# Four weight slots, the low part written over the raw block, and one conversion instruction per block and engine

## The reference

```python
mod = (silu(c) @ w_mod[i] + b_mod[i]).reshape(-1, 3, 3, D_MODEL)      # D_MODEL = 1024
def _sublayer(x, fn, mod_j, g, b, weight):
    shift, scale, gate = mod_j[:, 0, None, :], mod_j[:, 1, None, :], mod_j[:, 2, None, :]
    y = fn(x * (1 + scale) + shift)
    return _layernorm(DEEPNORM_ALPHA * x + weight * gate * y, g, b)
def _swiglu(h, w_in, w_out):
    gate, up = jnp.split(h @ w_in, 2, axis=-1)
    return (jax.nn.silu(gate) * up) @ w_out
```

## Time and profile before

| | us |
|---|---|
| median of the three runs | 3140.94 |
| the profiled execution | 3138.93 |
| its span | 3137.1 |
| TensorE busy (matmuls) | 2776.5 |
| VectorE busy | 2017.5 |
| GpSimd busy | 1389.1 |
| ScalarE busy | 1265.3 |

### The profile page before, as it was taken

One profiled execution on the slowest core, in us unless ns is written; L12 is line 12 of the kernel. 1 busy time (PEld: TensorE's weight loads), 2 busy tenths in 40 slices (PEclk: granted clock), 3 DMA queues, 4 the chain that ended last, 5 costly groups with the idle time before them and its releaser, 6 DMA issues.

```text
span 3137.1 us, 53378 instructions
## 1 busy us (share of the span) xinstructions
PE 2776.5 (89%) x20695; PEld 2656.6 (85%) x20695; DVE 2017.5 (64%) x2628; ACT 1265.3 (40%) x1667; POOL 1389.1 (44%) x1170
## 2 busy tenths in 40 slices
PE   3998889999976999999889999999879969779797
PEld 3998789999965999999764899999769969479797
DVE  6667776676658766666666666765876564764654
ACT  2444344344333444444332344443434434244443
POOL 0693958469383583793920079277670000000000
PEclk7998889999887898998975899899889989689898
DMA  8764557577472575764730377567445545034452
GB/s 298 252 249 144 189 202 252 202 240 260 148 247 71 198 254 180 255 256 158 235 120 0 108 254 267 176 231 271 151 142 173 176 155 177 14 111 131 134 185 83
DMA packets 357173, 576.21 MB, mean 184 GB/s; under 512 B 22256, under 2 KB 297899, under 8 KB 356907
## 3 DMA queue, kind: packets, MB, share of 16 engines
q1 hardware_dynamic: 357034, 574.29, 53.2%
HBM read 573.20 MB, written 1.05 MB: 183 GB/s over the span
## 4 chain that ended last, share of the span: by engine, by line
PE 70%; DVE 16%; issue 6%; POOL 4%; ACT 2%; DMA 1%; SPq 1%; DVEq 0%; POOLq 0%; ACTq 0%
PE ps L1553 64%; DVE wlo L1011 3%; POOL mod_acc L639 3%; PE ps L1873 1%; DVE acc L1126 1%; PE ps L1864 1%; DVE acc L1042 1%; DVE z L1142 1%; POOL mod_w L634 1%; ACT whi L654 1%; DVE std L1148 1%; DVE prob L1243 1%; PE ps L1694 1%; DVE hf L1155 1%; POOL mod_acc L630 1%
## 5 line engine op out<-in xcount | busy, mean ns | idle before, releaser
L1011 DVE TENSOR_TENSOR wlo<-raw,whi 128x1024 fp32r<-128x1024 f32 x804 | 1132.6, 1420 | 851.5 <-ACT whi L654 850.7
L654 ACT ACTIVATE whi<-raw 128x1024 fp32r<-128x1024 f32 x804 | 838.1, 1050 | 1227.9 <-PE ps L1553 1153.0
L1553 PE MATMUL ps<-H_hi,whi 128*128 128x256 f32 x4256 | 1230.3, 289 | 97.0 <-DVE H_lo L1160 37.6
L1553 PE MATMUL ps<-H_lo,whi 128*128 128x256 f32 x4256 | 1225.3, 288 | 0.0
L1553 PE MATMUL ps<-H_hi,wlo 128*128 128x256 f32 x4256 | 1224.3, 288 | 0.0
L1553 PEld LDWEIGHTS ps<-H_hi,whi 128*128 128x128 f32 x4256 | 839.6, 197 | 103.2 <-issue 85.3
L1553 PEld LDWEIGHTS ps<-H_lo,whi 128*128 128x128 f32 x4256 | 839.7, 197 | 0.1
L1553 PEld LDWEIGHTS ps<-H_hi,wlo 128*128 128x128 f32 x4256 | 838.8, 197 | 0.0
L639 POOL TENSOR_TENSOR mod_acc<-mod_acc,mod_w 128x512 f32<-128x512 f32 x462 | 792.3, 1743 | 0.0
L625 POOL TENSOR_TENSOR pool_tick<-cond 128x1 f32<-128x1 f32 x176 | 129.8, 738 | 952.9 <-DVE ax L1054 761.7
L1553 PE MATMUL ps<-A_hi,whi 128*128 (+1 forms) x1880 | 536.1, 285 | 16.0 <-DVE wlo L1011 12.9
(11 more groups left out here) (276 smaller groups left out, 2257.3 us busy)
## 6 DMA issues: line engine op xcount, KB each, us to landing
raw<-in_ffn_w_in_dram SPq DMA_DIRECT2D x176, 1024.0 KB, 5.1
mod_w<-in_w_mod_dram SPq DMA_DIRECT2D x180, 768.0 KB, 6.0
raw<-in_ffn_w_out_dram SPq DMA_DIRECT2D x88, 1024.0 KB, 6.5
raw<-in_w_gate_up_dram SPq DMA_DIRECT2D x22, 1024.0 KB, 5.1
raw<-in_ssm_w_in_dram SPq DMA_DIRECT2D x20, 1024.0 KB, 6.8
raw<-in_w_in_dram SPq DMA_DIRECT2D x14, 1024.0 KB, 5.0
raw<-in_diff_w_in_dram SPq DMA_DIRECT2D x12, 1024.0 KB, 7.0
raw<-in_w_down_dram SPq DMA_DIRECT2D x11, 1024.0 KB, 4.9
```

Source lines behind the costliest of these rows:

```text
L654: return nc.scalar.activation(dst, src, ACT.Copy)
L1011: tt(wlo[b % 2][:, r], raw[b % RAW][:, r], whi[b % 2][:, r].bitcast(F32), ALU.subtract).then_inc(w_lo, 1)
L1553: m = pe.matmul(out, l, r, start=first and i == 0, stop=last and i == 2, skip_group_check=rest)
```

## The change

- `raw`, `wlo` and `whi` now have four slots each; `wlo` i lies at the address of `raw` i, so the subtraction writes over its own input. The memory used is the same.
- ScalarE and VectorE convert a block with one instruction of its whole width (2048 columns, 1152 for the q blocks of MLA, 256 for dt). ScalarE no longer waits for products. TensorE waits once per block for the low part.
- The load of block b waits for TensorE's products of block b-4 (before: for VectorE's split of block b-4).
- The first two blocks of the next step are converted in the last turns of `projected`, ahead of the layer norm; `finish` and the conversions inside `dve_ln` and `dve_pre` are gone.
- Loads on SyncE are written out instead of looped, and the units of modulation have new places: `mod_rows` gives the turn behind whose load each unit stands. The loads of the next step's first blocks are no longer pulled ahead of the last units of a mixer.

```diff
+def mod_rows(kind):
+    if kind == "mla":
+        turns = [1, 1, 5, 6, 7, 8, 10] + 9 * [12]
+    elif kind == "diff":
+        turns = [1, 1] + [3 + 5 * j // 4 for j in range(8)] + 6 * [15]
+    elif kind == "ssm":
+        turns = [1, 1] + [2 + 3 * j // 2 for j in range(14)]
+    else:
+        turns = [1, 1] + [2 + 2 * j for j in range(14)]
...
-        whi = [at(f"whi{i}", [P, SLOT], room(4 * SLOT), F32R) for i in range(2)]
-        wlo = [at(f"wlo{i}", [P, SLOT], room(4 * SLOT), F32R) for i in range(2)]
+        wlo = [at(f"wlo{i}", [P, SLOT], base + 4 * SLOT * i, F32R) for i in range(RAW)]
+        whi = [at(f"whi{i}", [P, SLOT], room(4 * SLOT), F32R) for i in range(RAW)]
...
                 if b >= RAW:
-                    sp.wait_ge(w_lo, 2 * (b - RAW + 1) if it is None else 2 * (b - RAW + 1) + 8 * it)
+                    sp.wait_ge(products, plan.used[b - RAW][1])
...
+            def load_mod(sub, unit):
+                k, half = divmod(unit, 2)
+                u = UNITS * sub + unit
+                sp.wait_ge(mod_used, u - 1)
...
+                    nxt = st.args[0] + 1 if st.kind not in ("hyb", "xatt") else SUB * DEPTH
+                    after = mod_rows(st.kind) if nxt < SUB * DEPTH else {}
+                    blocks = [b for g in st.lin.values() for b in range(g.b, g.b + g.n)]
+                    for i, b in enumerate(blocks):
+                        if b >= 2:
+                            load(b)
+                        for unit in after.get(i, []):
+                            load_mod(nxt, unit)
...
-                for h in range(2):
-                    if b >= 2:
-                        u = plan.used[b - 2][h]
-                        act.wait_ge(products, u if it is None else 4 * upb * it + u)
-                    r = slice(h * HALF, min((h + 1) * HALF, width))
-                    copy(whi[b % 2][:, r], raw[b % RAW][:, r]).then_inc(w_hi, 1)
+                r = slice(0, plan.width[b])
+                copy(whi[b % RAW][:, r], raw[b % RAW][:, r]).then_inc(w_hi, 1)
...
-                for h in range(2):
-                    v = 2 * b + h + 1
-                    dve.wait_ge(w_hi, v if it is None else 8 * it + v)
-                    r = slice(h * HALF, min((h + 1) * HALF, width))
-                    tt(wlo[b % 2][:, r], raw[b % RAW][:, r], whi[b % 2][:, r].bitcast(F32), ALU.subtract).then_inc(w_lo, 1)
+                dve.wait_ge(w_hi, b + 1 if it is None else 4 * it + b + 1)
+                r = slice(0, plan.width[b])
+                tt(wlo[b % RAW][:, r], raw[b % RAW][:, r], whi[b % RAW][:, r].bitcast(F32), ALU.subtract).then_inc(w_lo, 1)
...
-                walk(dve, g, lambda i, it: None if it is None and i >= g.n - 2 else convert(g.b + i + 2, it), 1, 2)
+                walk(dve, g, lambda i, it: convert(g.b + i + 2, it), 1, 2)
```

More of the change, by code:

```diff
@@ L182 @@
 }
+UNITS = 2 * DC
+def mod_rows(kind):
[7 more added lines that the diff above has]
+        turns = [1, 1] + [2 + 2 * j for j in range(14)]
+    after = {}
+    for u, t in enumerate(turns):
+        after.setdefault(t, []).append(u)
+    return after
 class Step:
@@ L201, in __init__ @@
         self.mods = SUB * DEPTH
-        self.blocks = []
+        self.blocks, self.width = [], []
         self.used = []
@@ L228, in block @@
         self.blocks.append(loads)
+        self.width.append({"dt": DC * SSM_H, "q_up": QUP}.get(loads[0][0], SLOT))
         self.slot[b % RAW] += 16 * len(loads)
@@ L564, in _ @@
                         sp.dma_start(mod_first[u % ring], w).then_inc(first_loaded[u % ring], 16)
[L565 to L587, removed]
+                if st.kind in ("ffn", "mla", "diff", "ssm", "hyb", "xatt"):
+                    nxt = st.args[0] + 1 if st.kind not in ("hyb", "xatt") else SUB * DEPTH
[6 more added lines that the diff above has]
+                            load_mod(nxt, unit)
+                    if st.kind == "ffn" and st.args[0] == SUB * DEPTH - 1:
                         sp.wait_ge(s["mod_sum"], st.n["mod_sum"])
@@ L590, in _ @@
                         sp.dma_start(mem[:, :, :], A["mem_2"][0].rearrange("(t p) d -> p t d", p=P)).then_inc(second_loaded, 16)
[L591 to L605, removed]
                 if st.kind == "store":
@@ L654, in copy, with convert @@
                 return nc.scalar.activation(dst, src, ACT.Copy)
[L656 removed]
+            def convert(b, it=None):
                 if b >= NB:
@@ L776, in turn @@
                 def turn(i, it=None):
-                    convert(g.b + i + 2, it, 2)
+                    convert(g.b + i + 2, it)
                     if i % 2 == 0:
@@ L789, in projected @@
                 g = st.lin["out"]
-                walk(act, g, lambda i, it: None if it is None and i == g.n - 1 else convert(g.b + i + 2, it, 2), 1, 2)
-            def finish(g):
-                convert(g.b + g.n + 1)
+                walk(act, g, lambda i, it: convert(g.b + i + 2, it), 1, 2)
             def act_mla(st, n):
@@ L1506, in dve_pre @@
             def dve_pre(st, n):
-                g = steps[steps.index(st) - 2].lin["out"]
                 fold(n, "squared")
-                convert(g.b + g.n)
                 dve.wait_ge(s["std"], n["std"] + 1)
@@ L1612, in turn @@
                             xh, xl = (x[:, ds(it * 8 + k, 1), :].rearrange("p a n -> p (a n)") for x in (x_hi, x_lo))
-                        m = three(ybank(g, c), b % 2, h * HALF + c * P, P, xh, xl, k == 0 and c % 2 == 0, last and h == 1, rest=True)
+                        m = three(ybank(g, c), b % RAW, h * HALF + c * P, P, xh, xl, k == 0 and c % 2 == 0, last and h == 1, rest=True)
                         if last and h == 1 or not last and c == DC - 1:
```

55 lines of the change are left out of this document (21 added, 34 removed).

## The result

The kernel after takes 3210.95 us (median of four runs, 3206.66 to 3211.20) against 3140.63 beside it on the same chip. The ratio is 1.0225, with an interval of 1.0205 to 1.0244. The forecast was 3216, range 3165 to 3255. The profiled execution took 3206.66 us, its span is 3204.8, and the mean granted clock 0.896.

A forecast was written before the change was run, and what follows sets the result against it. In feed-forwards, most of the span, TensorE's unbroken matmuls were taken as the bound, so more slots gain nothing. Terms 67 + 3 + 4 - 9 - 2 + 12 = +75 on 3138.93 gave 3214, on the median 3216; range 3165 to 3255.

The forecast's parts named there:

- The hold at block 3: Feed-forwards: unit 2's wait, now ahead of load 3, stalls TensorE; 11.2 us in each of six, 67 us.
- Sublayer 0: First feed-forward: `ax` is ready early, so block 3 is only 3 us late; +3 (0 to 6).
- My reason about halves: Block 3 of feed-forwards: with whole-block conversions TensorE can't start on half a block any more.
- The layer norms: Reciprocal 1.4 us earlier, sums 1.8 later: net +0.4 for nine norms; together with last norm and `pre` steps, +4.
- MLA: Two MLA sublayers: GpSimd starts and runs earlier, next step's loads land later; -4.6 each, together -9 (-20 to +5).
- The other step: MLA's end: next step's two loads stand behind unit 15, so centred `z` comes at +8.6 instead of +3.5, +5.1.
- The differential mixer: Earlier start (-2.3) and earlier `ax` against conversions in series, GpSimd's pace holding as before; -2 (-10 to +8).
- The SSM: Hold 11 us, later loads meeting fewer units give some 4 back, whole-block xbc conversions cost 5; +12 (-5 to +25).
- The sum: Whole kernel: 67 + 3 + 4 - 9 - 2 + 12 = +75 us.
- half a hold: Rival: GpSimd slips ahead of the conversion or load 3 lands in 5 us; 3177, chance 0.21.
- more serial cost: Rival, also "the serial rival": whole-block conversions in series cost another 35 us in mixers and norms; 3250, chance 0.12.
- the third: Rival without a hold: unit 0 used by about T+6.2, feed-forwards cost nothing; 3135, chance 0.11.

The follow-up runs named there:

- experiment 5: Kernel after with feed-forward units 2 and 3 behind loads 5 and 7, the others two blocks apart from there: 3144.81 us, ratio 1.0025.
- experiment 4: Kernel before with only the feed-forwards' modulation units at the change's places: 3210.34 us, ratio 1.0234.
- experiment 1: Kernel after with feed-forward unit 2 behind load 4 instead of load 2: 3170.55 us, ratio 1.0116; second version, behind load 3: 3177.59 us, ratio 1.0136.
- experiment 6: Kernel after with both conversions in halves of 1024 columns and TensorE waiting for each half: 3178.92 us, ratio 1.0135.
- experiment 7: Kernel after with halves, the feed-forward turns of experiment 5 and new unit places in the SSM and MLA: 3100.45 us, ratio 0.9886.
- experiment 8: Kernel before with all modulation units placed as in experiment 7, no next-step loads pulled ahead: 3122.47 us, ratio 0.9962.
- the last edit: VectorE's conversion of the next step's second block moved behind the norm's last H_lo: 3179.19 us on experiment 1's first version, 3090.11 us on experiment 7.

## Why the prediction was right, step by step

**The hold at block 3: right, and close in size.** Its steps stand beside the measured ones of sublayer 3, as times after T: unit 0 used 14.7, measured 13.6; load 3 issued 15.3, measured 14.0; its transfer 7.5, measured 7.47; block 3 ready 27.5, started 27.3; wanted 19.0, measured 19.9 (670.08 less 7.40). The stall is 7.4 instead of 8.5, and the clock cost 2.6 instead of 2.7. Two errors compensate in part: unit 0 took 2.04 us and not the 3.00 of the earlier trace rows, and VectorE took 3.13 beside GpSimd and then 0.68 for `am`, which I had left out. Six of them were forecast at 67 us and measured at 58. Experiment 5 shows that the places of the units are all of it, and experiment 4 that they do it in either kernel. Sublayer 0 was put at +3; the table has 3.1 between the kernel after and experiment 5, and 4.4 over the kernel before. Unit 2 stood behind load 7 before the change, so with eight loads ahead of it, not seven.

GpSimd was held once, for the whole conversion: 1.94 us for an instruction that takes 0.20 alone. By the rule of the Trainium skill that the prediction weighed ("SBUF — State Buffer", section "SBUF: two separate sides") this is what had to come, and the trace agrees. My other evidence for it was misread. The 4.29 us of the earlier trace rows agree that the two engines exclude each other, but they are no wait for one instruction. VectorE ran four halves there without a pause, each some 1.2 us, and GpSimd waited for all four, which is more than the rule's one instruction:

```profile
638.54 4.62 DVE L1011 TENSOR_TENSOR wlo<-raw,whi 128x1024 fp32r<-128x1024 f32 x4
```

In the kernel after a single conversion stands in that place, since block 3 is late. Where two stand, GpSimd waits 4.14 us (experiment 1).

**My reason about halves was wrong, without effect on the sum.** I wrote that TensorE can't start on half a block any more. It couldn't before either, at this place: `am` holds the banks until both halves are done (experiments 4 and 6).

**The layer norms: right.** +0.4 each was forecast, and the feed-forwards of experiment 5 are within 0.7 us of before. The mechanism is there too: `z` begins behind the conversion of block n+1. In sublayer 2 of experiment 5, `z` begins at T+190.3 and the reciprocal at T+204.1, against T+188.4 and T+204.1 before: what `z` lost, the missing conversion gave back. In the kernel after, VectorE's timeline at the end of sublayer 2 (it answers to the earlier trace rows) goes straight from one to the other, and no conversion stands before the reciprocal any more:

```profile
622.47 2.29 DVE L989 TENSOR_TENSOR wlo<-raw,whi 128x2048 fp32r<-128x2048 f32 x1 [3.47 <-ACT whi L644]
624.68 1.26 DVE L1111 SCALAR_TENSOR_TENSOR z<-ps,gw,ax 128x256 f32<-128x256 f32 x3
...
638.11 1.75 DVE L1124 RECIPROCAL std<-std 128x256 f32<-128x256 f32 x1 [0.96 <-ACT std L733]
```

**MLA: wrong in sign, small.** -4.6 each was forecast, +1.5 measured. The first step that failed is "Now unit 7 follows the last load of the step itself: -6", after the 6.04 us of idle time before that unit. The idle time did not go, it moved to unit 2, which now stands behind load 5, and that load waits for the products of block 1. GpSimd still ended 5.1 us earlier (T+123.1 against T+128.1), of which 2.3 are its earlier start as forecast; I had 8.3. The other step went as written but cost 7.9 us where I had 5.1: the next step's loads land late and their conversions run beside GpSimd. GpSimd's, ScalarE's and VectorE's timelines (to the earlier trace rows):

```profile
300.27 0.20 POOL L615 TENSOR_TENSOR pool_tick<-cond 128x1 f32<-128x1 f32 x1 [6.13 <-DMA mod_w<-in_w_mod_dram]
...
397.35 3.80 POOL L629 TENSOR_TENSOR mod_acc<-mod_acc,mod_w 128x512 f32<-128x512 f32 x3
```
```profile
397.53 1.92 ACT L644 ACTIVATE whi<-raw 128x2048 fp32r<-128x2048 f32 x1 [13.80 <-DMA raw<-in_ffn_w_in_dram]
401.26 1.92 ACT L644 ACTIVATE whi<-raw 128x2048 fp32r<-128x2048 f32 x1 [1.81 <-DMA raw<-in_ffn_w_in_dram]
```
```profile
399.48 6.03 DVE L989 TENSOR_TENSOR wlo<-raw,whi 128x2048 fp32r<-128x2048 f32 x2 [11.32 <-ACT whi L644]
...
412.49 2.48 DVE L1120 SCALAR_TENSOR_TENSOR z<-ps,z 128x512 f32<-128x512 f32 x4 [1.31 <-PE ps L1629]
```

GpSimd ends at 401.15 and the centred `z` begins at 412.49, 11.3 us later; I had 8.6, and the earlier trace rows 3.5. With unit 2 one load earlier and halves, experiment 7 has both MLAs faster than before, by 1.7 and 2.1 us.

**The differential mixer: right in number, by luck.** -2 was forecast and -2.4 measured, but not by the path that I gave. The kernel before stood 6.88 us at block 9 (the stall of the earlier trace rows). That stall is gone, and two others are new: 3.41 us at block 4 and 4.86 at block 7 (TensorE's timeline):

```profile
914.28 0.41 PE L1525 MATMUL ps<-H_hi,whi 128*128 128x256 f32 x1 [4.86 <-DVE wlo L989]
```

**The SSM: right in sign, too high**, +12 forecast, +3.9 measured. The step that failed is the one on its later loads, "(two in three blocks, not one in each), which gives some 4 back". The parts can be read from the table. Halves against whole blocks are 8.8 (I had 5). Places against those of experiment 7 are 13.6, the hold at block 3 among them (TensorE stood 6.96 us at 1520.41). What is left is 18.5 us of gain over the kernel before where I had 4. Experiment 8 divides that gain: 10.3 us come from the places of the units alone, where I had 4 for the thinner ones, and 8.2 from the rest of the change, where I had nothing. The kernel before had a stall of 5.36 us at block 8 (experiment 8), which is gone in experiment 7, and I had read 59.24 of 65.00 us busy without asking what the rest was.

**The sum.** +75 was forecast; the spans of the profiled executions differ by 67.7, the medians by 70.3. By the spans, the holds were 9 lower and the SSM 8 lower, MLA 12 higher, and the rest within 4. That the sum is within 0.2% is helped by errors of both signs. Of the rivals, the totals of half a hold (3177) and of more serial cost (3250) are out. The mechanism of the serial rival is not: halves give back 26 us (experiment 6), of which the sum had 5, in the SSM. What hid the rest is a gain that the sum had at nothing: 22 us between experiments 7 and 8, from slots, aliasing or early conversions, with 1.0 to 2.3 us of it in five of the six later feed-forwards, where I had written that more slots can't gain a microsecond. That these two nearly cancel was luck. The condition of the third, unit 0 used by T+6.2, was missed by 7.4 us.

## What to carry to other kernels

- Before a transfer with a wait is moved forward in an in-order queue, compute when its wait ends, and look at every load behind it. Here unit 2's wait ended some 14 us into the sublayer. Behind load 7, and behind load 5 too, that cost nothing; behind load 2 it cost 58 us over six sublayers.
- A buffer's release event sets which places in the queue are possible. When a load's wait changes from "split" to "multiplied", what stood behind it must be placed anew.
- Judge such a change with the places chosen for each version. Here the same slots and early conversions come out 2.2% slower, or 1.1% faster with three other lists of turns and halves; the last edit lost 9 us in one arrangement and gained 10 in another.

## What the runs showed of the hardware that was not expected

A single 2048-column conversion took up to 8.09 us, 3.5 times its 2.29 us alone. VectorE's timeline in the SSM, then GpSimd's:

```profile
1588.21 8.09 DVE L989 TENSOR_TENSOR wlo<-raw,whi 128x2048 fp32r<-128x2048 f32 x1 [2.50 <-ACT whi L644]
```
```profile
1588.21 0.20 POOL L615 TENSOR_TENSOR pool_tick<-cond 128x1 f32<-128x1 f32 x1
1588.37 2.04 POOL L624 TENSOR_SCALAR mod_w<-mod_w,cond 128x512 f32<-128x512 f32 x3
1590.37 3.79 POOL L629 TENSOR_TENSOR mod_acc<-mod_acc,mod_w 128x512 f32<-128x512 f32 x3
```

GpSimd began in the same moment and ran seven instructions one behind the other, until 1594.2; VectorE ended 2.1 us after that, about its own length. It did not come between them. The other direction looks the same: GpSimd's first instruction took 4.29 us beside four halves that VectorE ran without a pause, 4.14 beside two whole conversions and 1.94 beside one (the account above and experiment 1). The longest conversion of 1024 columns was 4.41 us with halves in the kernel after (experiment 6), 3.17 in experiment 7, 4.84 in the kernel before and 5.10 in experiment 4. That the exclusion lets one engine run several instructions before the other's turn comes is what all these rows agree with; no run was made for it alone.
